# MLP chunks with seven-product matmuls: own slots and a new order for the weight factors at each border, GpSimd's low parts in halves

## The chip, the cores and the metric

The kernel runs on one core of a Trainium2 chip, as one program. The metric is the device time of an execution in microseconds; the time before is the median of three runs. Engines: TensorE (PE, its weight loads PEld), VectorE (DVE), ScalarE (ACT), GpSimd (POOL), SyncE (SP, whose queue issues all DMAs).

## The reference

Three transformer layers on 512 tokens of width 1024 in float32: a hybrid layer with a conv MLP, then two layers that end in the MLP that matters here, once each (l = 0, 1):

```python
h = h + sq_relu_mlp(rms_norm_2(h, norm_mlp_g[i]), mlp_w_in[i], mlp_w_out[i])   # 1024 -> 4096 -> 1024
```

that is relu(x @ w_in) squared, times w_out.

## The kernel before

Activations lie transposed, features on the 128 partitions and the 512 tokens along a row. Every float32 matmul is made of three in a reduced-precision format: each operand is split in a high part (rounded copy) and a low part (operand minus high part), and high x high, high x low and low x high are added in PSUM.

**Up stage.** The 4096 hidden features are done in 4 chunks of 8 tiles (`N_CH`, `KD`; e = 0 to 7 is the tile in its chunk, t its number in the whole program's list of weight tiles). A tile's weights (512 KB) come by DMA to `stage[:, e % 2]`; ScalarE makes `w_hi` (`split_hi`, L1501), GpSimd `w_lo` in four instructions (`split_lo`, L500); TensorE runs 16 matmuls with `w_hi` (L635, L636) and 8 with `w_lo` (L641) into bank e % 2. VectorE evicts it (L2903), ScalarE squares it (L2069), and the two make the hidden tile's factors.

**Down stage of a fast chunk.** Chunks n = 0, 1, 2 of each MLP (`N_FAST`) multiply back to the output with a seven-product scheme for 2 x 2 blocks (Winograd's form of Strassen's): output halves of a pair of output tiles, token halves of 256 columns. The hidden tile gives seven factors of 256 columns (B11, T1, B21, T2, B22, T3, T4; `fc_hi`, `fc_lo` in `arena[:, 0:14]` and `[:, 24:38]`), the weights seven (A11, S1, A12, S2, S4, S3, A22 in the order of use). A chunk has four quads (j = 0 to 3; q counts them all). Quad q's weights, two DMAs of 512 KB, lie in `prob` for even q and in `stage` for odd q, the same `stage` as the up tiles'. A product (`product`, L1422) is 8 matmuls with the high weight factor (L1439, L1440) and 4 with the low (L1448), of 256 columns. In quad 0 the order is A11, S1, then three quarters each of A12 and S2, their last quarters, S4, S3, A22, because the last quarter needs the factors of up tiles e = 6 and 7. Chunk n = 3 works in the plain way.

The high weight factors are ScalarE's: `quad_copy` (L2040) and `quad_high` (L2051). The sums that S1 to S4 need are VectorE's (`quad_sum`, L2866 to L2878, through two PSUM banks), and so are the low parts of S1 and S2 (L2884). The low parts of the other five are GpSimd's (`quad_low`, L542). Results are added to x by VectorE (`added`, L2940). S2, S4 and S3 accumulate on the bank of an earlier product without clearing it, so each must wait until that product was added (`product_added`). A factor has one slot: the first three in `v_split` and `arena[:, 14, 15, 38]`, the last four (S2, S4, S3, A22) in the up tiles' `w_hi` and `w_lo`.

**The order** is written out by hand for each engine, every engine running its list in order:
- SyncE, `mlp2_loads` (L398): for n > 0 it waits until all low parts of the last quads are done, loads tiles e = 0 to 3, then the first quad, then e = 4 to 7, then the later quads.
- GpSimd, `mlp2_splits` (L550): low parts of tiles 0 to 5, A11, A12, tiles 6, 7, then S4, S3, A22, then the later quads.
- ScalarE, `mlp2` (L2053): per tile e the high part of tile e + 2, the square, and the tile's high factors; the quad's copy, A11 and S1 after e = 4, A12 after e = 5, S2 and S4 after e = 6, S3 and A22 before e = 7; at the end of the chunk the high parts of the next chunk's tiles 0 and 1, each after a wait for products of the last quad.
- VectorE, `fast` (L2887): per tile eviction (L2903), subtractions (L2907; L2913, L2914, L2916) and low factors (L2893); the quad's four sums and two low parts after e = 4, 5, 6; then, per quad, seven additions with the next quad's sums among them.

Of the kernel before, what the change touches and what calls it, by code (L numbers as in the profile page):

```python
# [16 lines left out]
F32 = mybir.dt.float32  # L17
F32R = mybir.dt.float32r
ALU = mybir.AluOpType
ACT = mybir.ActivationFunctionType  # L20

P = 128
S = 512
D = 1024
KD = D // P
# [18 lines left out]
HS = S // 2  # L44
# [28 lines left out]
QUADS = KD // 2  # L73
N_PROD = 7
# [51 lines left out]
def program(nc, x_in, params, consts, buckets, swa_table, weights, pairs, tables, out):  # L126
    with ExitStack() as ctx:
# [20 lines left out]
        with nc.sbuf_tensor("ff_space", [P, 2 * KD, S], F32) as early_space:  # L148
            with nc.sbuf_tensor("z", [P, N_IN, S], F32) as z, nc.sbuf_tensor("qkv", [P, 2, 3, S], F32) as qkv, \
# [36 lines left out]
                   [w_hi[:, a, 4 * b:4 * b + 4].rearrange("p k c -> p (k c)") for a in range(2) for b in range(2)])  # L186
        slot_lo = ([arena[:, a] for a in (14, 15, 38)] +
                   [w_lo[:, a, 4 * b:4 * b + 4].rearrange("p k c -> p (k c)") for a in range(2) for b in range(2)])
# [187 lines left out]
        def _(sp):  # L376
# [21 lines left out]
            def mlp2_loads(l):  # L398

                for n in range(N_FAST):  # L400
                    t = T_MLP2[l] + KD * n
                    q = QUADS * (N_FAST * l + n)
                    if n:
                        sp.wait_ge(slot_low, 5 * q)
                        loads(t, t + 2)
                    loads(t + 2, t + 4)
                    if n == 0:
                        sp.wait_ge(xn_ready, KD * (4 + 2 * l))
                    for r in range(2):
                        quad_load(q, r)  # L410
                    loads(t + 4, t + 8)
                    for r in range(2):
                        sp.wait_ge(lo_ready, t + KD - 1 + r)
                        quad_load(q + 1, r)
                    for j in range(2, QUADS):
                        for r in range(2):
                            quad_load(q + j, r)
                sp.wait_ge(slot_low, 5 * QUADS * N_FAST * (l + 1))
                t = T_MLP2[l] + KD * N_FAST
                loads(t, t + 2 * KD)  # L420
# [73 lines left out]
        def _(pool):  # L494
# [44 lines left out]
            def quad_low(q, k, src):  # L539

                pool.wait_ge(slot_high, N_HIGH * q + k + 2)
                nc.gpsimd.tensor_tensor(slot_lo[k], src, slot_hi[k].bitcast(F32), ALU.subtract).then_inc(slot_low, 1)  # L542
# [7 lines left out]
            def mlp2_splits(l):  # L550

                for n in range(N_FAST):
                    t = T_MLP2[l] + KD * n
                    q = QUADS * (N_FAST * l + n)
                    split_los(t, t + 6)
                    quad_lows(q, (HI_A11, HI_A12))
                    split_lo((t + 6) // 2, 0)
                    split_lo((t + 6) // 2, 1)
                    pool.wait_ge(tile_done, t + KD - 1)
                    quad_lows(q, (HI_S4,))  # L560
                    pool.wait_ge(tile_done, t + KD)
                    quad_lows(q, (HI_S3, HI_A22))
                    for j in range(1, QUADS):
                        quad_lows(q + j, (HI_A11, HI_A12, HI_S4, HI_S3, HI_A22))
# [929 lines left out]
        def _(act):  # L1494
# [558 lines left out]
            def mlp2(l):  # L2053
                root(3 + 2 * l)
                for n in range(N_FAST):
# [3 lines left out]
                    for e in range(KD):  # L2059
# [3 lines left out]
                        if e == KD - 1:  # L2063
                            act.wait_ge(hi_free, t + KD)
                            act.wait_ge(lo_ready, t + KD)
                            quad_high(q, HI_S3)
                            quad_high(q, HI_A22)
# [14 lines left out]
                        if e == 4:  # L2082
                            quad_copy(q)
                            quad_high(q, HI_A11)
                            quad_high(q, HI_S1)
                        elif e == 5:
                            quad_high(q, HI_A12)
                        elif e == 6:
                            act.wait_ge(hi_free, t + KD - 1)
                            act.wait_ge(lo_ready, t + KD - 1)  # L2090
                            quad_high(q, HI_S2)
                            quad_high(q, HI_S4)
# [4 lines left out]
                    for p_ in range(2):  # L2097
                        act.wait_ge(product_done, N_PROD * (q + QUADS - 1) + (HI_S4 + 1 if p_ == 0 else N_PROD))
                        split_hi((t + KD) // 2, p_)
# [24 lines left out]
        def _(dve):  # L2124
# [761 lines left out]

            def fast(l, n):  # L2887
# [9 lines left out]
                for e in range(KD):  # L2897
# [14 lines left out]
                    else:  # L2912
                        dve.tensor_tensor(tmp[:, 2, HS:S], tmp[:, 1, HS:S], tmp[:, 0, HS:S], ALU.subtract).then_inc(u_ready, 1)  # L2913
                        dve.tensor_tensor(tmp[:, 3, 0:HS], tmp[:, 1, HS:S], tmp[:, 2, 0:HS], ALU.subtract).then_inc(u_ready, 1)  # L2914
# [3 lines left out]
                        f_low(i, F_B21, F_B22, tmp[:, 1])  # L2918
                        dve.wait_ge(ffh_ready, NF1 + u + 4)
                        f_low(i, F_T3, F_T4, flat_tmp[:, 5 * HS:8 * HS])  # L2920
                    if e == 4:
                        quad_sum(q, 0)
                        quad_sum(q, 1)
                        quad_sum(q, 2)
                    elif e == 5:
                        quad_sum(q, 3)
                        quad_low(q, HI_S1)
                    elif e == 6:
                        dve.wait_ge(tile_done, t + KD - 1)
                        quad_low(q, HI_S2)  # L2930
                for j in range(QUADS):
                    v, s = q + j, (q + j) % 2
                    x0, x1 = x[:, 2 * j], x[:, 2 * j + 1]
                    r1, r2, r5 = R1[s][:, 0:HS], R2, R5

                    def added(dst, src, k, before=None):
                        dve.wait_ge(product_done, N_PROD * v + k + 1)
                        if before is not None:
                            dve.wait_ge(product_added, N_PROD * v + before)
                        dve.tensor_tensor(dst, dst, src, ALU.add).then_inc(product_added, 1)  # L2940

                    more = j < QUADS - 1
                    added(x0[:, 0:HS], r1, HI_A11)
                    if more:
                        quad_sum(v + 1, 0)
                    added(x1[:, HS:S], r5, HI_S1)
                    if more:
                        quad_sum(v + 1, 1)
                        quad_sum(v + 1, 2)
                    added(x0[:, 0:HS], r2, HI_A12, 1)  # L2950
                    if more:
                        quad_sum(v + 1, 3)
                        quad_low(v + 1, HI_S1)
                    added(x0[:, HS:S], r1, HI_S2)
                    if more:
                        quad_low(v + 1, HI_S2)
                    added(x0[:, HS:S], r5, HI_S4, 4)
                    both = x1.rearrange("p (h s) -> p h s", h=2)
                    added(both, r1.rearrange("p (o s) -> p o s", o=1).broadcast_to([P, 2, HS]), HI_S3, 2)
                    added(x1[:, 0:HS], r2, HI_A22, 6)  # L2960
# [218 lines left out]
```

## Time and profile before

| | |
|---|---|
| time before, median of 3 runs | 1785.05 us (1784.31 to 1787.32) |
| profiled execution, its own time | 1787.28 us |
| its span | 1785.5 us |
| mean granted clock of TensorE, share of 2.4 GHz | 0.987 |
| busy PE, PEld | 1730.2 us (97%), 1447.0 us (81%) |
| busy DVE, ACT, POOL | 1002.0, 847.8, 947.9 us (56, 47, 53%) |
| DMA | 167.82 MB, mean 94 GB/s |

Spans of matmuls are modelled and overlap, so a busy share of 97% is an upper view; the weight loads (PEld) show gaps more sharply. A row of a timeline has the start in us from the span's start, the duration, engine, line, operation, output <- inputs, shape and count, and in brackets the engine's idle time before it with what ended it. A wait for several semaphores is put down to the one that came last by the profile, which is not always the true one. The first MLP's fast chunks lie from about 784 to 1066 us, the second's from about 1410 to 1700.

### The profile page before, as it was taken

Reading aid. Unit: us, or ns where it says so; the run is one execution under the profiler, and the core shown is the slowest. Engines: PE = TensorE matmul, PEld = TensorE weight load, DVE = VectorE, ACT = ScalarE, POOL = GpSimd, SP = SyncE. Lnnn points to the kernel's source line nnn. Section 1 sums busy time; section 2 is a strip of 40 time slices with the busy share of each in tenths; the row PEclk is TensorE's granted clock in tenths of the full one; section 3 lists DMA queues with packets and bytes.
Section 4 is the critical chain, followed back from the end, with each engine's and each line's share of the span. In section 5 each row is a group of like instructions: output and inputs, shape, how many; then the busy total and the mean of one; then the engine's idle time right before and its main releaser. Section 6 shows DMA issues by size and latency. Waiting matters only on the chain.

```text
span 1785.5 us, 26970 instructions
## 1 busy us (share of the span) xinstructions
PE 1730.2 (97%) x9185; PEld 1447.0 (81%) x9185; DVE 1002.0 (56%) x1977; ACT 847.8 (47%) x1434; POOL 947.9 (53%) x1107
## 2 busy tenths in 40 slices
PE   9999999999999999998989899999999989898998
PEld 7778888888887788887979798877777879796987
DVE  6775655555112555676565554577776765655553
ACT  6665655555222444254343434456564544434343
POOL 5534655555554343464546457655645745464574
PEclk9999999999999999999999999999999999999999
DMA  5221322332223222232222223332221422232232
GB/s 190 70 73 52 115 94 94 98 102 94 94 95 136 95 67 88 71 118 77 101 82 95 82 63 103 135 104 101 81 100 60 130 82 96 71 107 83 72 95 94
DMA packets 48655, 167.82 MB, mean 94 GB/s; under 512 B 5376, under 2 KB 6672, under 8 KB 48528
## 3 DMA queue, kind: packets, MB, share of 16 engines
q1 hardware_dynamic: 48272, 166.05, 28.6%
q8 instruction: 57, 0.93, 0.2%
q10 hardware_dynamic: 288, 0.52, 0.1%
q14 instruction: 38, 0.31, 0.1%
HBM read 164.31 MB, written 2.24 MB: 93 GB/s over the span
## 4 chain that ended last, share of the span: by engine, by line
PE 88%; DVE 4%; issue 3%; ACT 2%; POOL 1%; DMA 0%; SPq 0%; DVEq 0%; ACTq 0%; POOLq 0%
PE bank L733 17%; PE bank L641 8%; PE bank L635 7%; PE bank L636 7%; PE bank L1030 4%; PE bank L1031 4%; PE bank L1035 4%; PE bank L1439 4%; PE bank L1440 4%; PE bank L1448 4%; PE bank L751 2%; PE bank L757 2%; PE bank L752 2%; PE bank L1077 2%; PE bank L1083 2%
## 5 line engine op out<-in xcount | busy, mean ns | idle before, releaser
L500 POOL TENSOR_TENSOR w_lo<-stage,w_hi 128x256 fp32r<-128x256 f32 x936 | 735.4, 819 | 592.3 <-ACT w_hi L1501 341.4
L1501 ACT ACTIVATE w_hi<-stage 128x1024 fp32r<-128x1024 f32 x234 | 246.6, 1054 | 273.2 <-PE bank L636 73.3
L635 PE MATMUL bank<-xn_hi,w_hi 128*128 128x512 f32 x544 | 214.4, 394 | 0.0
L636 PE MATMUL bank<-xn_lo,w_hi 128*128 128x512 f32 x544 | 213.8, 393 | 0.0
L733 PE MATMUL bank<-xn_hi,w_hi 128*128 128x512 f32 x464 | 189.0, 407 | 0.0
L733 PE MATMUL bank<-xn_lo,w_hi 128*128 128x512 f32 x464 | 181.8, 392 | 0.0
L641 PE MATMUL bank<-xn_hi,w_lo 128*128 128x512 f32 x544 | 145.6, 411 | 29.9 <-POOL w_lo L500 29.9
L641 PEld LDWEIGHTS bank<-xn_hi,w_lo 128*128 128x128 f32 x544 | 108.0, 200 | 55.2 <-POOL w_lo L500 32.4
L1030 PE MATMUL bank<-xn_hi,w_hi 128*128 128x512 f32 x352 | 137.1, 389 | 0.0
L1031 PE MATMUL bank<-xn_lo,w_hi 128*128 128x512 f32 x352 | 137.0, 389 | 0.0
L2940 DVE TENSOR_TENSOR x<-x,bank 128x256 f32<-128x256 f32 (+1 forms) x168 | 76.6, 456 | 91.6 <-PE bank L1448 90.9
L733 PE MATMUL bank<-xn_hi,w_lo 128*128 128x512 f32 x464 | 123.9, 398 | 0.0
L635 PEld LDWEIGHTS bank<-xn_hi,w_hi 128*128 128x128 f32 x544 | 104.1, 191 | 21.9
L636 PEld LDWEIGHTS bank<-xn_lo,w_hi 128*128 128x128 f32 x544 | 103.7, 191 | 22.0
L1439 PE MATMUL bank<-arena,w_hi 128*128 128x256 f32 x384 | 98.7, 288 | 15.0 <-ACT v_split L2051 12.4
L733 PEld LDWEIGHTS bank<-xn_hi,w_hi 128*128 128x128 f32 x464 | 87.2, 188 | 25.1 <-issue 8.5
L733 PEld LDWEIGHTS bank<-xn_hi,w_lo 128*128 128x128 f32 x464 | 84.6, 188 | 22.8 <-issue 6.0
L733 PEld LDWEIGHTS bank<-xn_lo,w_hi 128*128 128x128 f32 x464 | 87.3, 188 | 16.0
L1440 PE MATMUL bank<-arena,w_hi 128*128 128x256 f32 x384 | 97.7, 286 | 0.0
L1439 PEld LDWEIGHTS bank<-arena,w_hi 128*128 128x128 f32 x384 | 74.8, 195 | 17.1 <-ACT v_split L2051 13.4
L2903 DVE SCALAR_TENSOR_TENSOR tmp<-bank,rstd 128x512 f32<-128x512 f32 x48 | 33.2, 692 | 97.8 <-PE bank L641 93.2
L1035 PE MATMUL bank<-xn_hi,w_lo 128*128 128x512 f32 x352 | 86.9, 389 | 0.0
(391 smaller groups left out, 3755.5 us busy)
## 6 DMA issues: line engine op xcount, KB each, us to landing
stage<-weights SPq DMA_DIRECT2D x235, 512.0 KB, 3.5
prob<-pairs SPq DMA_DIRECT2D x24, 512.0 KB, 4.3
stage<-pairs SPq DMA_DIRECT2D x24, 512.0 KB, 3.5
bias<-table SPq DMA_DIRECT2D x11, 896.0 KB, 5.4
out<-z SPq DMA_DIRECT2D x8, 256.0 KB, 2.1
x<-x_in SPq DMA_DIRECT2D x3, 512.0 KB, 7.6
bias<-swa_table SPq DMA_DIRECT2D x4, 256.0 KB, 4.0
con<-consts SPq DMA_DIRECT2D x1, 640.0 KB, 9.6
```

The source lines that it names most:

```text
L500: ins = nc.gpsimd.tensor_tensor(w_lo[:, p_, ks], stage[:, p_, ks], w_hi[:, p_, ks].bitcast(F32), ALU.subtract)
L635: pe.matmul(G[p_][:], w_hi[:, p_, k], hi[:, k], start=(first and k == ks[0]), stop=False)
L636: mm = pe.matmul(G[p_][:], w_hi[:, p_, k], lo[:, k], start=False, stop=False)
L641: mm = pe.matmul(G[p_][:], w_lo[:, p_, k], hi[:, k], start=False, stop=(last and k == ks[-1]))
L733: mm = pe.matmul(G[p_][:], (w_hi if i < 2 * KD else w_lo)[:, p_, k], (xn_lo if i < 2 * KD and i % 2 else xn_hi)[:, k], start=(i == 0), sto ...
L1030: pe.matmul(UP[bank][:], w_hi[:, p_, k], xn_hi[:, k], start=(k == 0), stop=False)
L1031: mm = pe.matmul(UP[bank][:], w_hi[:, p_, k], xn_lo[:, k], start=False, stop=False)
L1035: mm = pe.matmul(UP[bank][:], w_lo[:, p_, k], xn_hi[:, k], start=False, stop=(k == KD - 1))
L1439: pe.matmul(region, w, fc_hi[:, i, f], start=(fresh and i == 0), stop=False, skip_group_check=True)
L1440: pe.matmul(region, w, fc_lo[:, i, f], start=False, stop=False, skip_group_check=True)
L1501: act.activation(w_hi[:, p_], stage[:, p_], ACT.Copy).then_inc(hi_ready, 1)
L2940: dve.tensor_tensor(dst, dst, src, ALU.add).then_inc(product_added, 1)
```

## The change

The last four factors get slots of their own in `arena[:, 16:24]`, which is unused in this stage. SyncE loads the first quad of a chunk n > 0 ahead of the chunk's up tiles. ScalarE makes the first quad's high factors after tiles 2 to 5 (all seven) and no longer waits for products before the next chunk's tiles 0 and 1. VectorE makes the four sums after e = 2 and both low parts after e = 3, and adds A11 and S1 of the first quad inside tile e = 7. GpSimd takes A11 and A12 between tiles 4 and 5, S4 between 6 and 7, S3 and A22 after 7, and makes every low part as two instructions of 256 columns. The diff, without the removal of the old `added` helper and the reordering of its calls, which beyond the first quad's A11 and S1 stay in their order:

```diff
         slot_hi = ([v_split[:, a, b].rearrange("p t f -> p (t f)") for a, b in ((0, 0), (0, 1), (1, 0))] +
-                   [w_hi[:, a, 4 * b:4 * b + 4].rearrange("p k c -> p (k c)") for a in range(2) for b in range(2)])
-        slot_lo = ([arena[:, a] for a in (14, 15, 38)] +
-                   [w_lo[:, a, 4 * b:4 * b + 4].rearrange("p k c -> p (k c)") for a in range(2) for b in range(2)])
+                   [arena[:, a] for a in (16, 17, 18, 19)])
+        slot_lo = [arena[:, a] for a in (14, 15, 38, 20, 21, 22, 23)]
         FC_LO = 24
...
                     if n:
+                        for r in range(2):
+                            quad_load(q, r)
                         sp.wait_ge(slot_low, 5 * q)
...
                         sp.wait_ge(xn_ready, KD * (4 + 2 * l))
-                    for r in range(2):
-                        quad_load(q, r)
+                        for r in range(2):
+                            quad_load(q, r)
                     loads(t + 4, t + 8)
...
                 pool.wait_ge(slot_high, N_HIGH * q + k + 2)
-                nc.gpsimd.tensor_tensor(slot_lo[k], src, slot_hi[k].bitcast(F32), ALU.subtract).then_inc(slot_low, 1)
+                for c in (0, HS):
+                    ins = nc.gpsimd.tensor_tensor(slot_lo[k][:, c:c + HS], src[:, c:c + HS],
+                                                  slot_hi[k][:, c:c + HS].bitcast(F32), ALU.subtract)
+                ins.then_inc(slot_low, 1)
 
...
                     q = QUADS * (N_FAST * l + n)
-                    split_los(t, t + 6)
+                    split_los(t, t + 4)
+                    split_lo((t + 4) // 2, 0)
                     quad_lows(q, (HI_A11, HI_A12))
+                    split_lo((t + 4) // 2, 1)
                     split_lo((t + 6) // 2, 0)
+                    quad_lows(q, (HI_S4,))
                     split_lo((t + 6) // 2, 1)
-                    pool.wait_ge(tile_done, t + KD - 1)
-                    quad_lows(q, (HI_S4,))
-                    pool.wait_ge(tile_done, t + KD)
                     quad_lows(q, (HI_S3, HI_A22))
...
                             split_hi(t // 2 + i + 1, p_)
-                        if e == KD - 1:
-                            act.wait_ge(hi_free, t + KD)
-                            act.wait_ge(lo_ready, t + KD)
-                            quad_high(q, HI_S3)
-                            quad_high(q, HI_A22)
                         act.wait_ge(evac[p_], t // 2 + i + 1 - MLP2_SKIP[l])
...
                                            ACT.Copy).then_inc(ffh_ready, 1)
-                        if e == 4:
+                        if e == 2:
                             quad_copy(q)
                             quad_high(q, HI_A11)
+                        elif e == 3:
                             quad_high(q, HI_S1)
+                            quad_high(q, HI_A12)
+                            quad_high(q, HI_S2)
+                        elif e == 4:
+                            quad_high(q, HI_S4)
+                            quad_high(q, HI_S3)
                         elif e == 5:
-                            quad_high(q, HI_A12)
-                        elif e == 6:
-                            act.wait_ge(hi_free, t + KD - 1)
-                            act.wait_ge(lo_ready, t + KD - 1)
-                            quad_high(q, HI_S2)
-                            quad_high(q, HI_S4)
+                            quad_high(q, HI_A22)
                     for j in range(1, QUADS):
...
                     for p_ in range(2):
-                        act.wait_ge(product_done, N_PROD * (q + QUADS - 1) + (HI_S4 + 1 if p_ == 0 else N_PROD))
                         split_hi((t + KD) // 2, p_)
...
 
+            def add_product(q, k):
+
+                j, r1 = q % QUADS, R1[q % 2][:, 0:HS]
+                x0, x1 = x[:, 2 * j], x[:, 2 * j + 1]
+                dst, src = {HI_A11: (x0[:, 0:HS], r1), HI_S1: (x1[:, HS:S], R5), HI_A12: (x0[:, 0:HS], R2),
+                            HI_S2: (x0[:, HS:S], r1), HI_S4: (x0[:, HS:S], R5),
+                            HI_S3: (x1.rearrange("p (h s) -> p h s", h=2),
+                                    r1.rearrange("p (o s) -> p o s", o=1).broadcast_to([P, 2, HS])),
+                            HI_A22: (x1[:, 0:HS], R2)}[k]
+                before = {HI_A12: HI_A11, HI_S4: HI_S2, HI_S3: HI_S1, HI_A22: HI_S3}.get(k)
+                dve.wait_ge(product_done, N_PROD * q + k + 1)
+                if before is not None:
+                    dve.wait_ge(product_added, N_PROD * q + before + 1)
+                dve.tensor_tensor(dst, dst, src, ALU.add).then_inc(product_added, 1)
+
             def fast(l, n):
...
                         dve.tensor_tensor(tmp[:, 2, HS:S], tmp[:, 1, HS:S], tmp[:, 0, HS:S], ALU.subtract).then_inc(u_ready, 1)
+                        if e == KD - 1:
+                            add_product(q, HI_A11)
                         dve.tensor_tensor(tmp[:, 3, 0:HS], tmp[:, 1, HS:S], tmp[:, 2, 0:HS], ALU.subtract).then_inc(u_ready, 1)
...
                         f_low(i, F_B21, F_B22, tmp[:, 1])
+                        if e == KD - 1:
+                            add_product(q, HI_S1)
                         dve.wait_ge(ffh_ready, NF1 + u + 4)
                         f_low(i, F_T3, F_T4, flat_tmp[:, 5 * HS:8 * HS])
-                    if e == 4:
-                        quad_sum(q, 0)
-                        quad_sum(q, 1)
-                        quad_sum(q, 2)
-                    elif e == 5:
-                        quad_sum(q, 3)
+                    if e == 2:
+                        for i in range(4):
+                            quad_sum(q, i)
+                    elif e == 3:
                         quad_low(q, HI_S1)
-                    elif e == 6:
-                        dve.wait_ge(tile_done, t + KD - 1)
                         quad_low(q, HI_S2)
...
```

## Rows read from the trace of the kernel before

**Rows 1.** Waits of TensorE's weight loads: engine line, releaser, us, times, longest us.

```profile
PEld bank L641 <- POOL w_lo L500: 32.4, 6, 5.4
...
PEld bank L1439 <- ACT v_split L2051: 13.4, 6, 2.2
...
PEld bank L1439 <- ACT w_hi L2051: 3.2, 4, 0.8
```

**Rows 2.** Timeline of TensorE's weight loads, chunk n=1: start us, us [idle before].

```profile
873.80 0.55 PEld L1448 LDWEIGHTS bank<-arena,w_lo 128*128 128x128 f32 x4
...
907.91 1.77 PEld L641 LDWEIGHTS bank<-xn_hi,w_lo 128*128 128x128 f32 x8
...
918.71 3.06 PEld L641 LDWEIGHTS bank<-xn_hi,w_lo 128*128 128x128 f32 x8 [5.40 <-POOL w_lo L500]
...
934.57 0.19 PEld L1439 LDWEIGHTS bank<-arena,w_hi 128*128 128x128 f32 x1 [2.23 <-ACT v_split L2051]
...
938.67 0.19 PEld L1439 LDWEIGHTS bank<-arena,w_hi 128*128 128x128 f32 x1 [0.82 <-ACT w_hi L2051]
```

**Rows 3.** Timeline of GpSimd, the same stretch.

```profile
865.29 1.29 POOL L542 TENSOR_TENSOR w_lo<-v_tok,w_hi 128x512 fp32r<-128x512 f32 x1 [0.81 <-ACT w_hi L2051]
...
888.50 3.20 POOL L500 TENSOR_TENSOR w_lo<-stage,w_hi 128x256 fp32r<-128x256 f32 x4 [0.30 <-PE bank L641]
...
908.16 1.29 POOL L542 TENSOR_TENSOR arena<-prob,v_split 128x512 fp32r<-128x512 f32 x1 [5.58 <-ACT v_split L2051]
914.41 1.52 POOL L542 TENSOR_TENSOR arena<-prob,v_split 128x512 fp32r<-128x512 f32 x1 [4.96 <-ACT v_split L2051]
915.89 5.52 POOL L500 TENSOR_TENSOR w_lo<-stage,w_hi 128x256 fp32r<-128x256 f32 x8
...
929.93 1.29 POOL L542 TENSOR_TENSOR w_lo<-prob,w_hi 128x512 fp32r<-128x512 f32 x1
```

**Rows 4.** Windows at 1.2 GHz: length, busy PE PEld DVE ACT POOL (x), clock, DMA.

```profile
918.70:923.70 5.00, 4.98 (x12) 3.92 (x13) 0.69 (x1) 0.37 (x1) 2.72 (x4) 0.50 0.51 154
...
1029.60:1032.90 3.30, 3.28 (x15) 3.30 (x16) 2.49 (x6) 0.94 (x2) 0.99 (x1) 0.50 0.00 0
...
sum 35.80, PE 35.64 PEld 29.47 DVE 9.37 ACT 5.70 POOL 17.94; mean PE 4.46 PEld 3.68 DVE 1.17 ACT 0.71 POOL 2.24
```

**Rows 5.** Timeline of VectorE, chunk n=1.

```profile
890.15 0.95 DVE L2914 TENSOR_TENSOR tmp<-tmp 128x256 f32<-128x256 f32 x1
...
895.74 1.73 DVE L2893 TENSOR_TENSOR arena<-tmp,arena 128x256 fp32r<-128x256 f32 x2
899.27 0.69 DVE L2903 SCALAR_TENSOR_TENSOR tmp<-bank,rstd 128x512 f32<-128x512 f32 x1 [1.80 <-PE bank L641]
...
907.57 0.70 DVE L2866 TENSOR_TENSOR bank<-bank,prob 128x512 f32<-128x512 f32 x1
...
910.15 0.69 DVE L2903 SCALAR_TENSOR_TENSOR tmp<-bank,rstd 128x512 f32<-128x512 f32 x1 [0.56 <-PE bank L641]
...
930.02 1.49 DVE L2913 TENSOR_TENSOR tmp<-tmp 128x256 f32<-128x256 f32 x1 [0.70 <-ACT tmp L2069]
...
933.21 0.96 DVE L2893 TENSOR_TENSOR arena<-tmp,arena 128x768 fp32r<-128x768 f32 x1 [0.31 <-ACT arena L2080]
934.08 0.41 DVE L2940 TENSOR_TENSOR x<-x,bank 128x256 f32<-128x256 f32 x1
...
938.19 0.41 DVE L2940 TENSOR_TENSOR x<-x,bank 128x256 f32<-128x256 f32 x1
```

**Rows 6.** Timeline of ScalarE, tile e=5 of chunk n=1.

```profile
912.97 0.85 ACT L2080 ACTIVATE arena<-tmp 128x768 fp32r<-128x768 f32 x1 [0.62 <-DVE tmp L2916]
913.72 0.61 ACT L2051 ACTIVATE v_split<-prob 128x512 fp32r<-128x512 f32 x1
```

**Rows 7.** GpSimd's line L500: ns min/median/max, first and last start.

```profile
L500 POOL TENSOR_TENSOR w_lo<-stage,w_hi x936: 717/742/1650, 17.0 to 1768.9; 128x256 fp32r<-128x256 f32 x188
```

**Rows 8.** SyncE's queue of DMAs, chunk n=1.

```profile
881.99 1.24 SPq L396 DMA_DIRECT2D prob<-pairs  x2
```

More of the change, by code:

```diff
@@ L2918, in fast @@
                         f_low(i, F_B21, F_B22, tmp[:, 1])
+                        if e == KD - 1:
+                            add_product(q, HI_S1)
                         dve.wait_ge(ffh_ready, NF1 + u + 4)
                         f_low(i, F_T3, F_T4, flat_tmp[:, 5 * HS:8 * HS])
-                    if e == 4:
-                        quad_sum(q, 0)
-                        quad_sum(q, 1)
-                        quad_sum(q, 2)
-                    elif e == 5:
-                        quad_sum(q, 3)
+                    if e == 2:
+                        for i in range(4):
+                            quad_sum(q, i)
+                    elif e == 3:
                         quad_low(q, HI_S1)
-                    elif e == 6:
-                        dve.wait_ge(tile_done, t + KD - 1)
                         quad_low(q, HI_S2)
                 for j in range(QUADS):
[L2932 to L2940, printed above, removed]
+                    v = q + j
                     more = j < QUADS - 1
-                    added(x0[:, 0:HS], r1, HI_A11)
+                    if j:
+                        add_product(v, HI_A11)
                     if more:
                         quad_sum(v + 1, 0)
-                    added(x1[:, HS:S], r5, HI_S1)
+                    if j:
+                        add_product(v, HI_S1)
                     if more:
@@ L2949, in fast @@
                         quad_sum(v + 1, 2)
-                    added(x0[:, 0:HS], r2, HI_A12, 1)
+                    add_product(v, HI_A12)
                     if more:
@@ L2953, in fast @@
                         quad_low(v + 1, HI_S1)
-                    added(x0[:, HS:S], r1, HI_S2)
+                    add_product(v, HI_S2)
                     if more:
                         quad_low(v + 1, HI_S2)
[L2957 to L2960, printed above, removed]
+                    add_product(v, HI_S4)
+                    add_product(v, HI_S3)
+                    add_product(v, HI_A22)
             def mlp2(l):
```

## The prediction, made before the changed kernel was run

> **What bounds the kernel now.** I read the waits of TensorE's weight loads first. Three waits make up nearly all that TensorE loses in the two second-layer MLPs: 32.4 us in 6 waits for GpSimd's w_lo, 13.4 us in 6 and 3.2 us in 4 put down to ScalarE, 49.0 us in all [rows 1]. Six is the number of fast chunks, so each loses the same. The timeline of chunk n=1 of the first MLP shows where: 5.40 us ahead of 918.71, at the low-part matmuls of up tile e=6, then 2.23 us ahead of 934.57 (product S2 of the first quad) and 0.82 us ahead of 938.67 (its S3) [rows 2]. Between them TensorE runs back to back.
>
> GpSimd's timeline explains the first. After the low parts of tile e=5 it takes the quad's A11 and A12, and only then those of e=6 and e=7 [rows 3]. A11's goes at 908.16, but A12's high part comes from ScalarE behind the chain of tile e=5: GpSimd sits idle 4.96 us, starts A12 at 914.41 and the train of e=6 and e=7 at 915.89, where TensorE had wanted the first at 913.35 (907.91 plus 5.44, the pitch of tiles). The windows cut to the stretches at 1.2 GHz add the second part: after these waits the granted clock is 0.50 in eight stretches; TensorE is busy 35.64 us in them, so 17.8 us are lost against 2.4 GHz [rows 4]. Two of the eight (3.28 us, and one like it in the second MLP) follow the 2.23 us wait of chunk n=2; after the other four such waits the clock stayed up. Loss now: 49.0 + 17.8 = 66.8 us, or 11.1 per chunk.
>
> The 2.23 us wait is named for ScalarE, but S2 accumulates in the bank of A11's product and needs VectorE's addition of that. It stands at 934.08 to 934.49, behind the whole chain of tile e=7 [rows 5], and the load starts 0.08 us later. Likewise 0.82 us: S3 waits for the addition of S2 (938.19 to 938.60), which stands behind four sums and a low part.
>
> **The change, part by part.**
> The wait at e=6 goes. GpSimd now does A11 and A12 between e=4 and e=5, S4 between e=6 and e=7, and S3 and A22 after e=7; ScalarE makes the high parts at e=2 to e=5. Once e=5's low parts are done, e=6's follow at once, some 5 us ahead of their use. This takes away 32.4 us, and the half clock behind it: (35.64 - 2 x 3.28)/2 = 14.5 us.
>
> A smaller wait comes at e=5, since A12 stands ahead of it. By rows of chunk n=1: VectorE evicts tile e=3 at 899.27. Undisturbed, its chain puts ScalarE's last copy 2.82 us later (910.15 to 912.97 in tile e=5) and the next instruction 0.75 us on [rows 5, 6]; so S1's high part starts at 902.84, A12's at 903.34 and ends at 903.95. GpSimd's low part of A12 in two halves ends at 905.4, and four instructions at 0.69 (5.52 for 8) bring e=5's to 908.2, against 907.91 when TensorE wants them: 0.3 us. On top of it VectorE makes all four sums in e=2 (about 2.7 us at 0.70 each, less overlap). They start at 897.5, when e=2's low parts end, and so push the eviction of e=3 0.8 us back; and trains of four that meet VectorE's operations take 3.20 instead of 2.76: 0.5 us. I take 1.6 us, with 0.3 and 2.7 as ends (the upper if both delays double).
>
> The wait at S2 goes and that at S3 grows. A11's addition now stands behind e=7's first subtraction, its product being done by then; S1's stands behind the first low part. S2's first part no longer waits. The last low part (933.21 now) starts 0.7 us sooner: the subtraction that took 1.49 us against 0.45, while GpSimd worked from 929.93, finds GpSimd idle (gain 1.04), and one addition at 0.33 is added. It ends at 933.5, when S2's last quarter is due (928.21 + 5.40). Behind it come three sums, A12's addition, a sum, a low part, then S2's addition: 3.4 us to its start at 936.8, its end at 937.2. S3 is due at 935.4 without waits: 1.9 us (1.5 to 2.3) where 3.05 stood. Six borders: 18.3 becomes 11.4.
>
> The clock. The new waits, 1.6 and 1.9 us, are shorter than the 2.23 that brought it down 2 times in 6. I keep those two, 3.3 us; ends 0 and one per border, 6 x 1.64 = 9.8.
>
> The port. VectorE's operations with two SBUF operands and GpSimd's disturb each other here: a train of four takes 3.20 us where half a train of eight takes 2.76 [rows 3], and the subtraction at 890.15 takes 0.95 us [rows 5]. The Trainium skill (SBUF — State Buffer, Who interferes with whom) says that such a pair excludes each other for a whole instruction. By that rule each of the three VectorE operations of tile e=4 (0.42, 0.45, 0.45) would hold back the train of e=5 for its whole length, 1.3 us instead of the 0.44 of the rows; the wait at e=5 would be 2.4 and the sum 4.8 us higher, an estimate with that page. I go by the row.
>
> Halving costs GpSimd: 256 columns take 0.74 (median) and follow at 0.69, 1.43 for two, where 512 took 1.29 [rows 3, 7]: 0.14 us times 120 low parts, 17 us of GpSimd. It is hidden. In the down stage S4's low part of a quad ends at 866.58 and TensorE wants it at 873.80; five times 0.14 eats 0.7 of 7.2 us. With that cover gone it would cost up to 17 us. Only A12's 0.14 is on the path, and counted.
>
> SyncE's queue: at n=1 and 2 the first quad's two loads are issued at 881.99, behind four weight loads [rows 8]. They now go ahead of the wait for the last quad's low parts. Their buffers, prob, are free once quad 2 is done with them, a quad (7 x 1.44 = 10.1 us) earlier, so they are there some 30 us before ScalarE's copy at e=2 (about 896). Cost nothing; were they later than that, the copy would hold the weights of e=5 behind it on ScalarE.
>
> Own slots let the next chunk's high parts go without waiting for the last products. TensorE has no idle time there now (rows 1 have no such wait), so 0. The removed waits of ScalarE and GpSimd at e=6 and e=7 are worth nothing beyond the above.
>
> Sum: 6 x (1.6 + 1.9) = 21.0, plus 3.3, is 24.3 left of 66.8: a gain of 42.5 us. The profiled execution took 1787.28 us, so 1744.8; it stands 2.2 above the median of 1785.05, so **1742.6**. Its own ends: 6 x 1.8 = 10.8 left gives 1729, and 6 x 5.0 + 9.8 = 39.8 left gives 1758.
>
> **Rivals.**
> Hidden wholly: e=5's wait vanishes because GpSimd meets less of VectorE, and no wait lowers the clock. Left: 6 x 1.9 = 11.4; 1730. For it: undisturbed the excess is only 0.3 us.
>
> The wait only moves a tile earlier: GpSimd waits for A12 as it does now, and e=5 loses what e=6 lost, with its half clock. Only the 6 x 1.15 at S2 and S3 is gained: 1778. For it: A12 still stands ahead of a tile's low parts. Against it: e=5's are now free to start as soon as A12 is done, and the four high parts before it were moved two tiles up while GpSimd's place moved by one.
>
> VectorE is starved. GpSimd's e=7, S3 and A22 form a train of eight halves, 5.52 us. If that kept VectorE out, tile e=6's low factors would come 5.5 us late against some 3.0 us of slack, 2.5 us more at A11; with 2.7 at e=5 and 1.9 at S3, and 9.8 for the clock, 52 us are left: 1770. Against it: the subtraction at 890.15 got in during the train of 888.50, after 0.5 us.
>
> Slower: the place is again A12 ahead of e=5 on GpSimd. With the clock falling behind every such wait (14.5 us as now) and 11.4 at S3, the change loses once that wait passes (66.8 - 14.5 - 11.4)/6 = 6.8 us. At 8 us it would be 1792. It needs A12's high part some 6 us later than worked out, as a late load of the first quad on ScalarE's and VectorE's queues would make it; the loads have over 20 us to spare.
>
> No change: if the order of GpSimd were not what holds e=6, the time would stay within 0.2%, about what a measurement of this kernel can tell from no change. The idle 4.96 us ahead of 914.41 speaks against it.
>
> **How the numbers follow.** Forecast 0.70, hidden wholly 0.12, moved only 0.08, starved 0.05, slower 0.03, no change 0.02. The range 1730 to 1762 holds the forecast with its ends and most of the hidden case, and leaves out about 0.18. Faster by over 0.2%: 0.95; within: 0.02; slower: 0.03.
>
> **What would show it.** The waits of L641 for L500 should stand at e=5, below 3 us each; ahead of the first quad's S2 there should be none, ahead of its S3 1.5 to 2.3. Stretches at 1.2 GHz in the MLPs should be few and short, not six behind up tiles. VectorE's subtractions in tile e=7 should last 0.45 us. GpSimd's low parts should be 240 instructions at 0.74, with its busy time up by some 17 us. I am wrong if a wait at e=5 is above 3 us, if the clock falls once or more in each chunk, or if TensorE waits for low parts in quads 1 to 3.

## The result, and the profile after

The changed kernel takes 1741.42 us in the median of four executions against 1785.8: ratio 0.975, 95% interval 0.9731 to 0.9769, faster. One of the four took 6030.34 us and is left out of the ratio; no trace shows why, and the other three lie between 1740.81 and 1741.46. The forecast was 1742.6. The profiled execution took 1740.81 us, 46.5 less than the one before (1787.28).

The head of its page: the span, and the busy time of each engine. GpSimd's busy time rises by 25.2 us with 120 more instructions, VectorE's by 6.4; nearly all of it is hidden.

```profile
span 1739.0 us, 27036 instructions
...
PE 1712.0 (98%) x9185; PEld 1433.9 (82%) x9185; DVE 1008.4 (58%) x1977; ACT 847.8 (49%) x1434; POOL 973.1 (56%) x1227
```

The waits of TensorE's weight loads (line, releaser, us, times, longest). L645 is L641 of before, L1443 is L1439.

```profile
PEld bank L1443 <- ACT arena L2055: 11.2, 6, 1.9
PEld bank L645 <- POOL w_lo L501: 8.8, 6, 1.6
```

Against [rows 1] the 32.4 us at the up tiles are 8.8, and the 16.6 in the first quad are 11.2: 49.0 us have become 20.0. Windows over the fast chunks of the two MLPs, with the granted clock third from the end: it is 1.00 in both, where before eight stretches stood at 0.50 [rows 4], so the 17.8 us of clock are gone too. 49.0 + 17.8 - 20.0 = 46.8 us, against the 46.5 measured on the profiled executions.

```profile
784.00:1060.00 276.00, 267.75 (x1650) 241.00 (x1649) 173.56 (x286) 129.19 (x204) 174.56 (x227) 1.00 0.30 97
1370.00:1650.00 280.00, 271.82 (x1667) 244.32 (x1667) 180.33 (x296) 133.80 (x211) 177.74 (x231) 1.00 0.31 98
```

Chunk n=1 of the first MLP again, TensorE's weight loads. The wait stands at e=5 now and is 1.38 us; it was 5.40 at e=6 [rows 2]. It holds for four borders, and is 1.64 at the first chunk of each MLP. The only other one stands ahead of S3 at all six borders, 1.80 us once and 1.88 to 1.89 five times.

```profile
902.56 1.69 PEld L645 LDWEIGHTS bank<-xn_hi,w_lo 128*128 128x128 f32 x8 [1.38 <-POOL w_lo L501]
...
924.43 0.19 PEld L1443 LDWEIGHTS bank<-arena 128*128 128x128 f32 x1 [1.88 <-ACT arena L2055]
```

ScalarE: in tile e=3 the last copy of the tile's factors, and A12's high part; then the high part of tile e=7.

```profile
895.99 0.85 ACT L2079 ACTIVATE arena<-tmp 128x768 fp32r<-128x768 f32 x1 [0.62 <-DVE tmp L2932]
...
897.22 0.62 ACT L2055 ACTIVATE v_split<-prob 128x512 fp32r<-128x512 f32 x1
...
906.19 1.06 ACT L1505 ACTIVATE w_hi<-stage 128x1024 fp32r<-128x1024 f32 x1 [3.65 <-DMA stage<-weights]
```

GpSimd: A11, A12, then the train of e=5 and e=6 (8), S4, and S3 and A22 at the end.

```profile
890.59 1.50 POOL L544 TENSOR_TENSOR arena<-prob,v_split 128x256 fp32r<-128x256 f32 x2
897.92 1.45 POOL L544 TENSOR_TENSOR arena<-prob,v_split 128x256 fp32r<-128x256 f32 x2 [5.83 <-ACT v_split L2055]
899.32 6.15 POOL L501 TENSOR_TENSOR w_lo<-stage,w_hi 128x256 fp32r<-128x256 f32 x8
905.43 1.43 POOL L544 TENSOR_TENSOR arena<-v_tok,arena 128x256 fp32r<-128x256 f32 x2
...
910.67 2.60 POOL L544 TENSOR_TENSOR arena<-qkv,arena 128x256 fp32r<-128x256 f32 x2
913.23 1.44 POOL L544 TENSOR_TENSOR arena<-prob,arena 128x256 fp32r<-128x256 f32 x2
```

A narrower window (899.40 to 902.46) cuts that train after its fourth instruction, the last of e=5:

```profile
899.32 3.19 POOL L501 TENSOR_TENSOR w_lo<-stage,w_hi 128x256 fp32r<-128x256 f32 x4
```

TensorE wanted the low parts of e=5 at 901.18, which is 6.73 us before the 907.91 of the kernel before; by this shift the trace can be laid over the steps of the prediction. GpSimd still sits idle ahead of A12, but A12 comes two tiles earlier, and e=6's low parts are done at 905.47, 2.4 us before their use at 907.91. S3's pair takes 2.60 us where two halves alone take 1.44: there VectorE's chain of tile e=5 meets it. That chain is late. ScalarE stood 3.65 us for the load of tile e=7's weights, with the square of e=5 behind it, and VectorE evicts e=6 at 912.71, right behind the chain. TensorE does not wait for any of this, but VectorE is still a little behind at tile e=7: it evicts it at 915.78 without an idle moment before.

VectorE: its fourth sum and the eviction of tile e=3 behind it; the last two low-part instructions of tile e=5 and the eviction of e=6; then, in tile e=7, its eviction, the first subtraction, A11's addition, the last low part, and S2's addition.

```profile
892.75 0.69 DVE L2877 TENSOR_TENSOR v_tok<-prob,bank 128x512 f32<-128x512 f32 x1
893.35 0.68 DVE L2917 SCALAR_TENSOR_TENSOR tmp<-bank,rstd 128x512 f32<-128x512 f32 x1
...
910.03 2.64 DVE L2907 TENSOR_TENSOR arena<-tmp,arena 128x512 fp32r<-128x512 f32 x2
912.71 0.69 DVE L2917 SCALAR_TENSOR_TENSOR tmp<-bank,rstd 128x512 f32<-128x512 f32 x1
...
915.78 0.68 DVE L2917 SCALAR_TENSOR_TENSOR tmp<-bank,rstd 128x512 f32<-128x512 f32 x1
917.16 0.43 DVE L2927 TENSOR_TENSOR tmp<-tmp 128x256 f32<-128x256 f32 x1 [0.70 <-ACT tmp L2068]
917.50 0.41 DVE L2899 TENSOR_TENSOR x<-x,bank 128x256 f32<-128x256 f32 x1
...
919.63 0.96 DVE L2907 TENSOR_TENSOR arena<-tmp,arena 128x768 fp32r<-128x768 f32 x1
...
923.95 0.41 DVE L2899 TENSOR_TENSOR x<-x,bank 128x256 f32<-128x256 f32 x1
```

The subtraction next to A11's addition takes 0.42 to 0.43 us; in [rows 5] it took 1.49. The last low part ends at 920.59, 4.81 us after the tile's eviction, where the prediction had 4.9.

GpSimd's low weight factors by form (ns min/median/max): 0.74 us each in the median, as worked out; the 1.46 us are the meetings with VectorE.

```profile
L544 POOL TENSOR_TENSOR arena<-prob,v_split x48: 736/740/797, 804.0 to 1619.0; 128x256 fp32r<-128x256 f32 x48
...
L544 POOL TENSOR_TENSOR arena<-qkv,arena x48: 732/743/1456, 823.6 to 1632.6; 128x256 fp32r<-128x256 f32 x48
```

### The profile page after: what moved, and what is told of

It is laid out like the page before. It is cut to its first block, busy times and chain, and to the rows that moved or that the text cites. A ratio compares the mean times of both kernels' runs of the same rounds, so it can differ in the third digit from the quotient of the medians.

```text
span 1739.0 us, 27036 instructions
## 1 busy us (share of the span) xinstructions
PE 1712.0 (98%) x9185; PEld 1433.9 (82%) x9185; DVE 1008.4 (58%) x1977; ACT 847.8 (49%) x1434; POOL 973.1 (56%) x1227
## 4 chain that ended last, share of the span: by engine, by line
PE 83%; DVE 7%; issue 3%; ACT 3%; POOL 2%; DMA 1%; SPq 0%; DVEq 0%; POOLq 0%; ACTq 0%
PE bank L737 18%; PE bank L639 5%; PE bank L640 5%; PE bank L645 5%; PE bank L1034 5%; PE bank L1035 5%; PE bank L1039 5%; PE bank L1443 4%; PE bank L1452 4%; PE bank L1444 4%; PE bank L755 3%; PE bank L761 3%; PE bank L756 3%; PE bank L1082 2%; PE bank L1081 2%
## 5 line engine op out<-in xcount | busy, mean ns | idle before, releaser
L645 PE MATMUL bank<-xn_hi,w_lo 128*128 128x512 f32 x544 | 135.8, 391 | 6.3 <-POOL w_lo L501 6.3
L645 PEld LDWEIGHTS bank<-xn_hi,w_lo 128*128 128x128 f32 x544 | 101.7, 188 | 29.7 <-POOL w_lo L501 8.8
L737 PE MATMUL bank<-xn_hi,w_lo 128*128 128x512 f32 x464 | 123.9, 398 | 0.0
L1452 PE MATMUL bank<-arena 128*128 128x256 f32 x672 | 109.9, 283 | 0.0
L1443 PE MATMUL bank<-arena 128*128 128x256 f32 x384 | 97.2, 285 | 10.1 <-ACT arena L2055 10.1
L737 PEld LDWEIGHTS bank<-xn_hi,w_lo 128*128 128x128 f32 x464 | 84.6, 188 | 22.8 <-issue 6.0
L1444 PE MATMUL bank<-arena 128*128 128x256 f32 x384 | 96.5, 283 | 0.0
L1452 PEld LDWEIGHTS bank<-arena 128*128 128x128 f32 x672 | 93.6, 192 | 0.0
L1039 PE MATMUL bank<-xn_hi,w_lo 128*128 128x512 f32 x352 | 86.9, 389 | 0.0
```

The source lines that it names most:

```text
L645: mm = pe.matmul(G[p_][:], w_lo[:, p_, k], hi[:, k], start=False, stop=(last and k == ks[-1]))
L737: mm = pe.matmul(G[p_][:], (w_hi if i < 2 * KD else w_lo)[:, p_, k], (xn_lo if i < 2 * KD and i % 2 else xn_hi)[:, k], start=(i == 0), sto ...
L1039: mm = pe.matmul(UP[bank][:], w_lo[:, p_, k], xn_hi[:, k], start=False, stop=(k == KD - 1))
L1443: pe.matmul(region, w, fc_hi[:, i, f], start=(fresh and i == 0), stop=False, skip_group_check=True)
L1444: pe.matmul(region, w, fc_lo[:, i, f], start=False, stop=False, skip_group_check=True)
L1452: mm = pe.matmul(region, w, fc_hi[:, i, f], start=False, stop=(i == QUADS - 1), skip_group_check=True)
```

## The experiments

All kernels but the fourth start from the changed kernel (1741.42 us). The profile lines named are each kernel's own; times are medians of four executions, for the fourth kernel of ten. They were taken in three sets beside the kernel before, which took 1786.78, 1785.54 and 1786.9 us in them; so a difference of about 1 us between kernels of different sets says little by itself, and the waits in the traces carry it.

### Whole low parts again

```diff
-for c in (0, HS):
-    ins = nc.gpsimd.tensor_tensor(slot_lo[k][:, c:c + HS], src[:, c:c + HS], ...)
-ins.then_inc(slot_low, 1)
+nc.gpsimd.tensor_tensor(slot_lo[k], src, slot_hi[k].bitcast(F32), ALU.subtract).then_inc(slot_low, 1)
```

> The changed kernel with GpSimd's low weight factors again as one instruction of 512 columns; the rest of the change stays. Theory (the gain is the order at the borders, the halves are hidden): 1741 us, between 1739 and 1744; the wait at up tile e=5 changes by less than 0.3 us. Rival (the halves are what lets VectorE in): 1747 us or more, with waits ahead of the first quad's products grown by over 1 us each.

1741.2 us. The waits are 11.3 us in the first quads and 7.9 at e=5, where they were 11.2 and 8.8. The 0.9 us at e=5 is the 0.14 us per border that A12's two halves cost, times six; it does not show in the median. The halves bring nothing here. GpSimd is busy 957.5 us, 15.6 less than in the changed kernel: that is what the halves cost it.

### A11 and S1 added late

```diff
 dve.tensor_tensor(tmp[:, 2, HS:S], ...)
-if e == KD - 1:
-    add_product(q, HI_A11)
...
-if j:
-    add_product(v, HI_A11)
+add_product(v, HI_A11)
```

and the same for S1.

> The changed kernel with the first quad's additions of A11 and S1 back behind the whole chain of tile e=7. Theory: the wait ahead of S2 comes back at 1.2 to 2.1 us and S3's shrinks from 1.88 to some 0.8, together 1.1 us more at each of six borders: 1748 us (1745 to 1750). Rival (S3 waits for VectorE anyway, so the early additions only move a wait): 1741 us.

1743.14 us, between the two. Weight loads of chunk n=1: 1.43 us ahead of S2 and 0.81 ahead of S3 stand where 1.88 stood.

```profile
903.15 1.69 PEld L645 LDWEIGHTS bank<-xn_hi,w_lo 128*128 128x128 f32 x8 [1.37 <-POOL w_lo L501]
...
921.32 0.19 PEld L1443 LDWEIGHTS bank<-arena 128*128 128x128 f32 x1 [1.43 <-ACT v_split L2055]
...
925.43 0.19 PEld L1443 LDWEIGHTS bank<-arena 128*128 128x128 f32 x1 [0.81 <-ACT arena L2055]
```

So the early additions bring 0.36 us at this border, some 2 us in all (the waits differ by 2.0 us, the medians by 1.7). The wait ahead of S2 was 2.23 us; the change brings it to 1.43 without them, because GpSimd no longer holds the subtraction of tile e=7, which takes 0.43 us here and took 1.49. I had put 1.1 us on their absence, from an upper end of 2.1 for S2; the time came out below the range given.

### Loads and ScalarE's waits put back

```diff
 if n:
-    for r in range(2):
-        quad_load(q, r)
     sp.wait_ge(slot_low, 5 * q)
...
 if n == 0:
     sp.wait_ge(xn_ready, KD * (4 + 2 * l))
+for r in range(2):
+    quad_load(q, r)
...
 for p_ in range(2):
+    act.wait_ge(product_done, N_PROD * (q + QUADS - 1) + (HI_S4 + 1 if p_ == 0 else N_PROD))
     split_hi((t + KD) // 2, p_)
```

> The changed kernel with two parts taken back that the prediction costed at nothing: the first quad's loads stand behind the loads of up tiles 0 to 3 again, and ScalarE's two high parts at a chunk's end wait for the last quad's products again. Theory: 1741.4 us within 1.5. Rival (the loads come too late for the copy at e=2, or the next chunk's first tile waits): over 1746 us, with a wait at e=2 to 5 or at e=0.

1741.0 us. The changed kernel issues the first quad's two loads of chunk n=1 from 849.99 on,

```profile
849.99 3.17 SPq L395 DMA_DIRECT2D prob<-pairs  x2
```

and here they are issued from 875.79 on, some 13 us ahead of the copy at e=2 (889.4 in the changed kernel):

```profile
875.79 1.27 SPq L395 DMA_DIRECT2D prob<-pairs  x2
```

Both parts cost and bring nothing, as predicted.

### The kernel before with halves only

```diff
-nc.gpsimd.tensor_tensor(slot_lo[k], src, slot_hi[k].bitcast(F32), ALU.subtract).then_inc(slot_low, 1)
+for c in (0, HS):
+    ins = nc.gpsimd.tensor_tensor(slot_lo[k][:, c:c + HS], src[:, c:c + HS], ...)
+ins.then_inc(slot_low, 1)
```

> The kernel before with GpSimd's low weight factors in halves and nothing else. Theory: VectorE's subtraction in tile e=7 that took 1.49 us is blocked for half as long, the wait ahead of S2 (2.23 us) shrinks by some 0.5 us at six borders: 1783 us (1780 to 1787). Rival (the halves carry much of the gain): below 1775 us.

1787.26 us against 1786.78: the same (ratio 1.0003, 0.9993 to 1.0012), and not the 3 us less that I expected. The wait ahead of S2 fell only from 2.23 to 2.14 us, and that at e=6 grew from 5.40 to 5.54. The mechanism that I expected is half there. VectorE's three subtractions of tile e=7 and its first addition behind them:

```profile
932.63 0.43 DVE L2916 TENSOR_TENSOR tmp<-tmp 128x256 f32<-128x256 f32 x1 [0.70 <-ACT tmp L2072]
932.97 0.96 DVE L2917 TENSOR_TENSOR tmp<-tmp 128x256 f32<-128x256 f32 x1
933.97 0.84 DVE L2919 TENSOR_TENSOR tmp<-tmp 128x256 f32<-128x256 f32 x1
...
936.60 0.41 DVE L2943 TENSOR_TENSOR x<-x,bank 128x256 f32<-128x256 f32 x1
```

GpSimd at that time:

```profile
931.28 1.44 POOL L543 TENSOR_TENSOR w_lo<-qkv,w_hi 128x256 fp32r<-128x256 f32 x2 [1.52 <-PE bank L644]
932.68 1.85 POOL L543 TENSOR_TENSOR w_lo<-prob,w_hi 128x256 fp32r<-128x256 f32 x2
```

The first subtraction is free (0.43 for 1.49), but the second (0.96) and the third (0.84) are each held by a half: 0.97 us lost where one block lost 1.04. Cutting the instruction in two made each block shorter and doubled their number; the chain that met them paid the same.

### A12's low part after tile e=5

```diff
 split_lo((t + 4) // 2, 0)
-quad_lows(q, (HI_A11, HI_A12))
+quad_lows(q, (HI_A11,))
 split_lo((t + 4) // 2, 1)
+quad_lows(q, (HI_A12,))
 split_lo((t + 6) // 2, 0)
```

> The changed kernel with GpSimd taking the low part of A12 after those of tile e=5, not before. Theory (the wait at e=5 is A12 standing ahead of it): the six waits of 1.4 to 1.6 us go, 8.8 us in all, and e=6 has over 3 us in hand: 1732.6 us (1731 to 1735). Rival (GpSimd is short of time there, the wait moves to e=6): 1740 to 1742 us.

1731.75 us, 9.7 less than the changed kernel: 8.8 of waits at e=5, and 0.9 ahead of S3, where the wait is 1.71 us in place of 1.88. All that is left among the waits for another engine in these stages:

```profile
PEld bank L1444 <- ACT arena L2056: 10.3, 6, 1.7
```

The wait at e=5 is gone, and none came at e=6.

### S2 added ahead of the next quad's sums

```diff
+if j == 0:
+    quad_sum(v + 1, 1)
+    add_product(v, HI_A12)
+    add_product(v, HI_S2)
+    quad_sum(v + 1, 2)
+    quad_sum(v + 1, 3)
+    quad_low(v + 1, HI_S1)
```

for j = 0, in place of the old order; the other quads keep theirs.

> The changed kernel with VectorE's additions of A12 and S2 of the first quad ahead of the next quad's third and fourth sums and low part. Theory (S3's wait of 1.88 us is S2's addition standing behind them): the wait falls below 0.3 us, 10 to 11 us less: 1731 us (1729 to 1733). Rival (the sums are as urgent; the wait moves into the second quad): 1740 to 1743 us.

1729.75 us, 11.7 less. What is left is e=5's:

```profile
PEld bank L645 <- POOL w_lo L501: 8.8, 6, 1.6
```

### Both

> Both at once: A12's low part after tile e=5 and S2's addition first. Theory: the two waits are independent, 20 us less than the changed kernel: 1721.5 us (1720 to 1725). Rival (each hides the other's): 1728 us or more.

1721.3 us: ratio 0.964 to the kernel before (0.9624 to 0.9656), 20.1 us less than the changed kernel. None of the named waits is left in either MLP. The head of its page:

```profile
span 1719.6 us, 27036 instructions
...
PE 1709.5 (99%) x9185; PEld 1434.3 (83%) x9185; DVE 1013.4 (59%) x1977; ACT 845.9 (49%) x1434; POOL 973.5 (57%) x1227
```

This version beats both kernels.

### GpSimd's order of before, high parts early

```diff
-split_los(t, t + 4)
-split_lo((t + 4) // 2, 0)
+split_los(t, t + 6)
 quad_lows(q, (HI_A11, HI_A12))
-split_lo((t + 4) // 2, 1)
 split_lo((t + 6) // 2, 0)
-quad_lows(q, (HI_S4,))
 split_lo((t + 6) // 2, 1)
+pool.wait_ge(tile_done, t + KD - 1)
+quad_lows(q, (HI_S4,))
+pool.wait_ge(tile_done, t + KD)
 quad_lows(q, (HI_S3, HI_A22))
```

> The changed kernel with GpSimd's order of before (A11 and A12 after tile e=5's low parts, S4, S3 and A22 behind tile e=7's with their two waits for tiles), while the high parts stay early at e=2 to 5. Theory (the 5.40 us at e=6 came from A12's high part being late, not from its place in GpSimd's list): no wait at e=5 nor at e=6; GpSimd's last three low parts now fall on VectorE's chain of tile e=7 and lengthen it by up to 1 us: 1736 us (1731 to 1742). Rival (the place in the list alone made the wait): a wait of over 3 us at e=6 and 1770 us or more.

1735.77 us: 5.6 us faster than the changed kernel. There is no wait at e=5 or e=6. Weight loads of chunk n=1:

```profile
919.10 0.19 PEld L1443 LDWEIGHTS bank<-arena 128*128 128x128 f32 x1 [0.42 <-issue]
...
922.83 0.19 PEld L1443 LDWEIGHTS bank<-arena 128*128 128x128 f32 x1 [1.88 <-ACT arena L2055]
```

The 1.88 ahead of S3 stays, and 0.42 appears at S2's last quarter, because GpSimd's last low parts meet tile e=7's chain again. So the place of A11 and A12 in GpSimd's list did not make the 5.40 us by itself: with the high parts early it does no harm. GpSimd's idle 4.96 us in [rows 3] ended with A12's high part, and that is the late one. No run moves A12's high part alone, without the other six and the new slots, so how much of the change the 5.40 us needed is not shown. Moving A12 ahead of e=5 is the part of the change that costs (A12's low part after tile e=5, above, gives 9.7 us).

### Only the slots and the early high parts

The order of GpSimd as just shown, the late additions, the whole low parts and the loads put back as above, all at once.

> Only the own slots and the early sums and high parts of the change: GpSimd's order of before, whole low parts, the late additions of A11 and S1 and the first quad's loads behind tiles 0 to 3; the wait for products at a chunk's end stays away. Theory (these carry all of the gain at e=6): no wait at e=5 and e=6, 2.2 us at S2 and 0.8 at S3, which is 18 us where the changed kernel has 20: 1740 us (1738 to 1745). Rival (the order on GpSimd carries it): 1765 us or more.

1741.72 us. The waits are nearly those of [rows 1] without L641's:

```profile
PEld bank L1438 <- ACT v_split L2050: 13.4, 6, 2.2
...
PEld bank L1438 <- ACT arena L2050: 2.4, 3, 0.8
```

1741.72 against the 1786.9 of the kernel before in that comparison is 45.2 us, as much as the whole change gains (44.4 against 1785.8). The rest of it nets to nothing: GpSimd's new order costs 5.6 us, and the early additions, with the halves and the loads, bring 6.0 with the old order (1741.72 to 1735.77). Only 2.0 of the 6.0 are waits. Most of the rest is clock: three of the six 2.23 us waits here are followed by a stretch at 1.2 GHz, and in the kernel shown just before there is none.

```profile
sum 10.23, PE 10.23 PEld 10.23 DVE 9.13 ACT 4.44 POOL 2.92; mean PE 3.41 PEld 3.41 DVE 3.04 ACT 1.48 POOL 0.97
```

TensorE is busy for 10.23 us in the three (windows from 920.57, 1517.90 and 1606.64), which costs 5.1 us in the profiled execution.

### A12's low part three times, and twice

```diff
 pool.wait_ge(slot_high, N_HIGH * q + k + 2)
+if k == HI_A12 and q % QUADS == 0:
+    for spare in (flat_bias[:, 0:S], flat_bias[:, S:2 * S]):
+        for c in (0, HS):
+            nc.gpsimd.tensor_tensor(spare[:, c:c + HS], src[:, c:c + HS], ...)
```

The second has one spare buffer. Both add work and leave none out.

> The changed kernel with two more low parts of A12 (four instructions of 256 columns, written to a spare buffer) ahead of the one that counts, in each first quad: the wait at e=5 goes from 1.4 to 1.6 us to about 4.3. Theory (a long wait costs its own length and a stretch at 1.2 GHz behind it, as the 5.40 us did): 16.8 us for the waits and some 2 us of clock at most of the six, 1770 us (1764 to 1776), with granted clock 0.50 behind them. Rival (only its own length): 1758 us and no stretch at 1.2 GHz.

> The same with one more low part of A12 (two instructions), the wait at e=5 about 2.9 us. Theory (waits of this size lower the clock at some of the borders, as 2.23 us did in 2 of 6): 8.4 us for the waits and 0 to 5 for the clock, 1750 to 1755 us. Rival (waits this short never lower it unless one at 5.4 us went before): 1749.8 us and no stretch at 1.2 GHz.

Three times: 1769.62 us. The wait at e=5:

```profile
PEld bank L650 <- POOL w_lo L501: 26.2, 6, 4.6
```

It is 4.27 to 4.56 us long at six borders, and a stretch at 1.2 GHz follows it six times out of six. Two of them (window, busy times, then clock, DMA share, GB/s):

```profile
910.30:915.50 5.20, 5.14 (x12) 4.08 (x13) 0.69 (x1) 1.45 (x2) 4.48 (x8) 0.50 0.57 173
1002.50:1007.70 5.20, 5.16 (x12) 4.09 (x13) 0.69 (x1) 1.50 (x2) 4.51 (x7) 0.50 0.53 161
```

The waits for other engines are 16.5 us longer than in the changed kernel (17.4 more at e=5, 0.9 less in the quads), and the median is 28.2 higher: 11.7 us of clock, 2 per border.

Twice: 1753.25 us.

```profile
PEld bank L650 <- POOL w_lo L501: 18.3, 6, 3.2
```

The clock fell at 2 of the six waits of 2.91 to 3.20 us, both of 3.20, while one of 3.17 left it up:

```profile
817.10:820.30 3.20, 3.14 (x8) 2.51 (x9) 0.00 (x0) 0.00 (x0) 3.20 (x6) 0.52 0.52 161
1420.90:1424.40 3.50, 3.44 (x8) 2.77 (x9) 0.00 (x0) 0.00 (x0) 3.50 (x7) 0.51 0.45 150
```

Waits for other engines are 9.3 us longer and the median 11.8 higher, which leaves 2.5 us for the clock; half of the 6.58 us that TensorE is busy in these two windows gives 3.3.

### Both moves with whole low parts

The version with both moves, with the first experiment's edit.

> The version with A12's low part after tile e=5 and S2's addition first, and with GpSimd's low weight factors again as one instruction each. Theory (the halves bring nothing and cost nothing): 1721.3 us within 1. Rival (they help once the other waits are gone): 1724 us or more.

1721.69 us: the halves do nothing there either.

## Why the prediction was right

The time was 1.2 us off. Point by point:

**The wait at e=6 and its clock.** Predicted to go whole, 32.4 + 14.5 us; it did. The reason given was mixed: GpSimd's order and A12's high part being late. The runs separate them in part. The early sums and high parts in their own slots do it without the new order; the new order is not needed and costs 5.6 us. The new order without the early high parts was not run.

**The wait at e=5.** Predicted 1.6 us with ends 0.3 and 2.7; measured 1.38 four times and 1.64 twice. With the shift of 6.73 us the steps fall where they were put: the eviction of e=3 at 893.35 (893.3), A12's low part at 897.92 (898.0). The eviction was late by the fourth sum, as worked out. The low parts of e=5 took 3.19 us (899.32 to 902.51) where four undisturbed take 2.76: 0.43 us, the 0.44 of [rows 3] again, which the step had rounded to 0.5. The three terms unrounded are 0.25, 0.8 and 0.44, 1.5 us in all, and A12's low part started 0.1 earlier than forecast. The 0.43 us are far from the 1.3 us for the train in the estimate with the Trainium skill's page (SBUF — State Buffer, Who interferes with whom). That one engine waits for the other agrees with the traces: before, the subtraction that started at 930.02 lasted 1.49 us and ended 0.29 us behind GpSimd's instruction beside it [rows 3, 5]. But what a meeting costs GpSimd's train is not the whole VectorE operation: the third instruction of e=5 took 0.93 us and the fourth 0.91, against 0.74 alone, some 0.2 us each where VectorE's operation takes 0.42 to 0.45.

**S2 and S3.** Predicted 3.05 to 1.9; measured 3.05 to 1.88 in chunk n=1, with S2's addition 8.17 us behind the eviction of e=7 both in the forecast (936.8 less 928.63) and in the trace (923.95 less 915.78). The share of the early additions was never priced by itself; it is 0.36 of the 1.17 us at this border (3.05 less 1.88), and the rest is GpSimd's absence from tile e=7. The eviction of e=7 itself is some 0.17 us late in the changed kernel, for the wait ahead of S3 is 1.71 us where A12's low part is out of the way. The prediction's "18.3 becomes 11.4" takes 3.05 us for all six borders, where [rows 1] have 16.6 in all; its sum goes by the 66.8 us that hold the 16.6, so the forecast is not touched.

**The clock.** This is the term that was mis-sized: two drops, 3.3 us, were kept and none came. With waits at e=5 of 1.4 instead of 1.6 this makes the left-over 20.0 us instead of 24.3, and the gain 46.5 on the profiled executions where 42.5 was forecast. So the sum was 4.0 us off, and that the median came within 1.2 us is in part luck: the forecast took off 2.2 us because the profiled execution before stood that far above its median, and the one after stood 0.6 below its own.

**Halves, loads, waits at a chunk's end.** Costed at nothing, with the cover named; all three measured as nothing. The halves' 17 us on GpSimd were right: they are 15.6 us in the changed kernel (973.1 against 957.5 without them) and 18.7 in the kernel before (966.6 against 947.9). The other 9.6 of the 25.2 us come with the rest of the change, in whose order GpSimd meets VectorE more, as in S3's pair. All lie hidden but A12's 0.14 us per border.

**The rivals.** "Only moved", "starved" and "slower" are excluded by the trace. Something of "starved" is there: at 910.03 VectorE's last two low-part instructions of tile e=5 take 2.64 us together where they took 0.68 and 0.96 in tile e=7 of the kernel before (at 932.22 and 933.21), but no product waits for it. "No change" had its condition wrong: GpSimd's order was indeed not what held e=6, and the time still fell by 2.5%, because the change moved the high parts as well. "Hidden wholly" was not what happened, but is what the move of A12 past tile e=5 makes (1731.75 against the 1730 given to it).

What stays open: why 1.64 and not 1.38 us at the first chunk of each MLP, whether A12's high part alone would have been enough, and what decides which of several equal waits lowers the clock.

## What to carry to other kernels

Follow a wait back through the in-order lists of all engines to the operand that is late, and move that one up first; here what stands behind it needed no new order, and the new order cost 5.6 us. An instruction that must wait for a late operand goes behind those that are ready (A12 behind e=5: 9.7 us) and an addition that frees a PSUM bank goes ahead of work with slack (S2's: 11.7 us). A wait of TensorE is priced with the clock behind it: here 5.40 us cost about 7.8.

## What was not expected of the hardware

Cutting GpSimd's instruction in two in the kernel before did not free VectorE, since two consecutive operations of VectorE were blocked instead of one (0.97 us for 1.04). And the clock falls after waits of TensorE by their length, not at one sharp length: of the waits of 1.4 to 1.9 us in the changed kernel none lowered it (0 of 12), and none under 2 us did in any other run; of those of 2.14 us 1 of 6 did in the kernel before with halves, of those of 2.23 us 2 of 6 in the kernel before and 3 of 6 with the slots and early high parts only, of 2.9 to 3.2 us 2 of 6, of 4.3 to 4.6 us 6 of 6, of 5.4 us 6 of 6 in the kernel before, and of 5.5 us 6 of 6 in the kernel before with halves.
